# A two-layer encoder trunk with hierarchical MoE: the layer's first unit beside the ten weight slots, routing in one pass, and column halves for the last two down units

## What is computed

```python
def hierarchical_moe(h, norm_g, w_group, b_group, w_router, b_router, w_gate_up, w_down):
    xt = rms_norm(h, norm_g).reshape(B * S, D)
    g_prob = softmax(xt @ w_group + b_group)            # 4 groups
    g_idx = argmax(g_prob); g_w = g_prob[g_idx]
    e_logits = (xt @ w_router + b_router).reshape(-1, 4, 8)[g_idx]
    top_p, top_i = top_k(softmax(e_logits), 2)          # two experts of that group
    top_p = top_p / sum(top_p)
    gates = one_hot(g_idx * 8 + top_i) * (g_w * top_p)
    for each of the 32 experts:
        a, b = split(xt @ w_gu)                         # w_gu 1024 x 1024
        acc += ((silu(a) * b) @ w_d) * g                # w_d  512 x 1024
```

## Time and profile before

| | |
|---|---|
| median of 3 runs | 1136.43 us (1135.44 to 1140.93) |
| the profiled execution, its own time | 1138.69 us |
| its span in the profile | 1136.9 us |
| mean granted clock of TensorE, share of full | 0.976 |
| busy: PE, DVE, ACT, POOL | 89%, 21%, 15%, 5% |
| read from memory | 428.94 MB |
| largest groups of PE | L899 (gate and up) 2048 records, L933 (down) 1024 records |

### The profile page before, as it was taken

The page is one execution under the profiler, slowest core; times in us unless marked ns, Lnnn a source line. Parts: engine busy times, 40 slices in busy tenths (PEclk is TensorE's granted clock), DMA queues, the critical chain, the costliest instruction groups (busy, mean ns, idle before and its releaser), DMA issues.

```text
span 1136.9 us, 11377 instructions
## 1 busy us (share of the span) xinstructions
PE 1009.1 (89%) x4810; PEld 437.8 (39%) x4810; DVE 240.7 (21%) x527; ACT 171.1 (15%) x430; POOL 60.2 (5%) x94
## 2 busy tenths in 40 slices
PE   7999998989797989879799999979898989797986
PEld 6884532323232323223264654332323223232321
DVE  6992420101010010101035614101010101010101
ACT  3865300100000000000044503000000000000000
POOL 2890000000000000000000000000000000000000
PEclk9999999999999999999999999999999999899999
DMA  9794699999999999999996656999999999999996
GB/s 312 208 361 159 233 425 426 429 426 429 427 429 427 427 430 426 429 426 428 405 370 215 206 189 272 429 428 428 427 429 425 429 427 428 427 429 428 428 421 261
DMA packets 65006, 430.72 MB, mean 379 GB/s; under 512 B 12102, under 2 KB 22429, under 8 KB 44220
## 3 DMA queue, kind: packets, MB, share of 16 engines
q1 hardware_dynamic: 64830, 429.86, 92.8%
q10 hardware_dynamic: 126, 0.14, 0.0%
HBM read 428.94 MB, written 1.05 MB: 378 GB/s over the span
## 4 chain that ended last, share of the span: by engine, by line
PE 49%; DMA 45%; SPq 2%; ACT 1%; DVE 1%; issue 1%; DVEq 0%
DMA ring<-in_w_gate_up_dram 17%; DMA ring<-in_w_down_dram 15%; PE bank L899 12%; PE bank L933 10%; DMA zone<-in_w_gate_up_dram 10%; PE bank L789 5%; PE bank L880 5%; DMA zone<-in_w_down_dram 4%; PE bank L948 3%; PE bank L1130 2%; PE bank L829 2%; SPq L420 2%; PE bank L1027 1%; PE bank L1049 1%; PE bank L801 1%; PE bank L1004 1%
## 5 line engine op out<-in xcount | busy, mean ns | idle before, releaser
L899 PE MATMUL bank<-ring,zone 128*32 128x512 f32 x1184 | 336.0, 612 | 48.9 <-DMA ring<-in_w_gate_up_dram 30.8
L899 PE MATMUL bank<-zone 128*32 128x512 f32 x864 | 266.7, 611 | 33.4 <-DMA zone<-in_w_gate_up_dram 18.5
L933 PE MATMUL bank<-ring,xT 128*32 128x512 f32 x704 | 169.4, 622 | 20.0 <-DMA ring<-in_w_down_dram 14.3
L899 PEld LDWEIGHTS bank<-ring,zone 128*32 128x32 f32 x1184 | 87.7, 113 | 233.5 <-issue 233.1
L899 PEld LDWEIGHTS bank<-zone 128*32 128x32 f32 x864 | 68.3, 112 | 152.1 <-issue 152.1
L1348 DVE TENSOR_TENSOR xT<-xT,bank 128x512 f32<-128x512 f32 x16 | 11.0, 687 | 486.3 <-PE bank L899 486.3
L933 PE MATMUL bank<-zone,xT 128*32 128x512 f32 x320 | 96.3, 593 | 4.9 <-ACT xT L640 2.4
L1353 DVE TENSOR_TENSOR h<-bank,h 128x512 f32<-128x512 f32 x64 | 44.2, 691 | 259.6 <-PE bank L948 259.6
L638 ACT ACTIVATE xT<-bank 128x512 f32<-128x512 f32 x16 | 9.6, 597 | 563.5 <-PE bank L899 563.5
L933 PEld LDWEIGHTS bank<-ring,xT 128*32 128x32 f32 x704 | 44.7, 113 | 109.7 <-issue 90.3
L880 PEld LDWEIGHTS bank<-zone,xn 128*128 128x128 f32 x512 | 58.4, 192 | 13.3 <-issue 13.3
(11 more groups left out here) (247 smaller groups left out, 627.8 us busy)
## 6 DMA issues: line engine op xcount, KB each, us to landing
ring<-in_w_gate_up_dram SPq DMA_DIRECT2D x74, 2048.0 KB, 36.1
zone<-in_w_gate_up_dram SPq DMA_DIRECT2D x54, 2048.0 KB, 36.3
ring<-in_w_down_dram SPq DMA_DIRECT2D x44, 2048.0 KB, 36.7
zone<-in_w_down_dram SPq DMA_DIRECT2D x20, 2048.0 KB, 36.8
ring<-in_a_pw_w_dram SPq DMA_DIRECT2D x8, 1024.0 KB, 11.9
ring<-in_a_pw_w_dram SPq DMA_DIRECT2D x2, 2048.0 KB, 11.2
ring<-in_w_o_dram SPq DMA_DIRECT2D x2, 2048.0 KB, 20.9
ring<-in_w_uq_dram SPq DMA_DIRECT2D x1, 2304.0 KB, 13.0
```

Of the source, the lines that this page charges most:

```text
L899: ins = nc.tensor.matmul(bank[b][s * CAP:(s + 1) * CAP, :], xs[:, k, s * CAP:(s + 1) * CAP], rhs[:, b * HALF:(b + 1) * HALF], start=(k == ...
L933: ins = nc.tensor.matmul(bank[2 + b][s * CAP:(s + 1) * CAP, :], hidT[:, k, s * CAP:(s + 1) * CAP], rhs[:, b * HALF:(b + 1) * HALF], start= ...
```

## The change

- **The first unit outside the slots.** Unit 0 of each layer (the first 4 KB piece of the rows of all four experts) is loaded into four other places of 1024 columns: two in `xT`, `y_sb`, and a new tile `spare`. Unit 10 takes its slot and is issued in its place; the order is 10, 1 to 9, 0. Before unit 0 SP waits for the logits. DVE waits for the use of unit 0 before it writes to `xT`. `spare` also holds, at other times, what had tiles of its own: taps of the convolution, mask, router weights of layer 0, small arrays of the attention. The mask is now written by POOL in the attention, and DVE waits for it.
- **Units 4 to 11 of quad 0 by blocks** instead of by rows.
- **Routing.** Group logits lie as a fifth row of eight beside the four groups' experts (padded with a very low number). One pass finds the best of each of the five rows, a second one the second best of the four groups; the group's one-hot then selects. The first quad's one-hot is made from the places without the subtraction. The five keep-awake matmuls become 3 in layer 0 and 4 in layer 1.
- **The end of a layer.** The last quad's units 10 and 11 are each loaded in two column halves of 1 MB (pieces of 2 KB), both first halves before both second ones. The PE takes the first half of the columns of both, then unit 10's second half, scatters the first half, then unit 11's second half, and scatters that. In every quad the scatter goes by column halves first. Norm and transposes behind layer 0 and the first product of the attention follow the order of halves.

The core of the diff:

```diff
+        AHEAD = [SLOTS] + list(range(1, SLOTS)) + [0]
...
-        def by_blocks(n):
-            return n != 0
+        def by_blocks(n, u):
+            return n != 0 or u >= 4
...
+        first_unit = [xT_flat[:, 0:D], xT_flat[:, D:2 * D], y_sb, spare[:, :]]
...
+            def tail_dma(l, u, ex, hf):
+                r0 = (u - GU) * P
+                src = a["w_down"][l][bass.ds(ex, SIDE), r0:r0 + P, hf * HALF:(hf + 1) * HALF].rearrange("e p c -> p e c")
+                sp.dma_start(unit_sb[slot_last(l, u)][:, :, hf * HALF:(hf + 1) * HALF], src
+                             ).then_inc(E[l]["tail_in"] if hf == 0 else E[l]["unit_in"][slot_last(l, u)], 16)
...
-                for g in range(EARLY):
-                    if g < SLOTS:
-                        first(g)
+                for g in AHEAD + list(range(SLOTS + 1, EARLY)):
+                    if g == 0:
+                        sp.wait_ge(logits_done, 2 * l + 2)
+                        for s in range(SIDE):
+                            src = a["w_gate_up"][l][s, 0:HALF, :].rearrange("(p k) c -> p k c", k=4)[:, 0, :]
+                            sp.dma_start(first_unit[s], src).then_inc(first_in, 16)
+                        continue
+                    if g <= SLOTS:
+                        first(g % SLOTS)
...
+                        if u < UNITS - 2:
+                            unit_dma(l, slot_last(l, u), u, (i + (QUADS - 1)) % QUADS * SIDE, u < GU)
+                    for hf in range(2):
+                        for u in (UNITS - 2, UNITS - 1):
+                            tail_dma(l, u, (i + (QUADS - 1)) % QUADS * SIDE, hf)
...
-                keep_awake(5)
+                keep_awake(3 + l)
...
+                        if first and half == 0:
+                            for k in range(4):
+                                unit = landed(k)
+                                sides = unit if k == 0 else [unit[:, s, :] for s in range(SIDE)]
+                                chunk(sides, k, range(SIDE)).then_inc(e["used"], 1)
+                            continue
...
+                def down_last(n, landed, i):
+                    pe.wait_ge(e["hidT_ready"], n + 1)
+                    for k in range(KF - 2):
+                        unit = landed(GU + k)
+                        for b in range(2):
+                            ins = down_rows(k, b, unit)
+                        ins.then_inc(e["used"], 1)
+                    pe.wait_ge(e["tail_in"], 32 * i + 32)
+                    for k in (KF - 2, KF - 1):
+                        ins = down_rows(k, 0, unit_sb[slot_last(l, GU + k)])
+                    ins.then_inc(e["half_done"], 1)
+                    down_rows(KF - 2, 1, landed(UNITS - 2)).then_inc(e["used"], 1)
+                    scatter(n, 0)
+                    down_rows(KF - 1, 1, landed(UNITS - 1)).then_inc(e["used"], 1)
+                    scatter(n, 1)
...
-                link(V.tensor_reduce(gmx[:, :], lg[:, :, 0:G], AX_X, ALU.max))
-                V.tensor_tensor(gex[:, :, :], lg[:, :, 0:G], over(gmx[:, :], G), ALU.subtract).then_inc(gexp_in, 1)
-                link(V.tensor_tensor(geq[:, :, :], lg[:, :, 0:G], over(gmx[:, :], G), ALU.is_equal))
...
+                def top_of(values, top, hit, index, hot, n):
+                    im = iota_m[:, 0:EG].unsqueeze(1).to_broadcast([P, n, EG])
+                    link(V.tensor_reduce(top, values, AX_X, ALU.max))
+                    link(V.tensor_tensor(hit, values, over(top, EG), ALU.is_equal))
+                    link(V.tensor_tensor(hit, hit, im, ALU.mult))
+                    link(V.tensor_reduce(index, hit, AX_X, ALU.min))
+                    link(V.tensor_tensor(hot, im, over(index, EG), ALU.is_equal))
...
+                top_of(rows(lg[:, :, :, :]), row(mx[:, :, :]), rows(seq[:, :, :, :]), row(eix[:, :, :]), rows(oh1[:, :, :, :]), NRW)
+                link(V.scalar_tensor_tensor(out=em[:, :, :, :], in0=oh1[:, :, 0:G, :], scalar=-2 * NEG, in1=lg[:, :, 0:G, :],
+                                            op0=ALU.mult, op1=ALU.add))
...
+                top_of(rows(em[:, :, :, :]), row(mx2[:, :, :]), by_group(eeq), ix2, by_group(oh2), NGR)
...
+                link(V.tensor_tensor(picked_by_group, oh1[:, :, 0:G, :], oh2[:, :, :].rearrange("p t (g x) -> p t g x", g=G), ALU.add))
+                V.tensor_tensor(picked_by_group, picked_by_group, oh1[:, :, G, 0:G].unsqueeze(3).to_broadcast([P, TT, G, EG]),
+                                ALU.mult).then_inc(mask_ready, 1)
+                V.tensor_tensor(gex[:, :, :], lg[:, :, G, 0:G], over(mx[:, :, G], G), ALU.subtract).then_inc(exp_in, 1)
+                V.tensor_tensor(vm[:, 0, :, :], mx[:, :, 0:G], oh1[:, :, G, 0:G], ALU.mult)
+                link(V.tensor_tensor(vm[:, 1, :, :], mx2[:, :, :], oh1[:, :, G, 0:G], ALU.mult))
...
-                link(V.tensor_scalar(slot[:, :, 0:NE], eeq[:, :, :], -1.0, None, ALU.add))
...
+                    numbers, at = (iota_1, eeq) if first else (iota, slot)
...
-                    if not first:
+                    if first:
+                        dve.wait_ge(e["used"], 1)
+                    else:
                         dve.wait_ge(e["back_done"], n)
```

More of the change, by code:

```diff
@@ L662, in _ @@
             last = experts(0)
-            norm(2, E[0]["s_added"], 4 * last)
-            for b in range(4):
-                act.wait_ge(xT_ready, 8 + b + 1)
+            norm(2, E[0]["s_added"], 4 * last, (3, 4))
+            for i, b in enumerate(BY_HALF):
+                act.wait_ge(xT_ready, 8 + i + 1)
                 t, kh = b // 2, b % 2
@@ new lines, in gate_up, with chunk @@
+                def gate_up(n, landed, first):
+                    def chunk(rhs, k, sides):
+                        for b in range(2):
+                            for s in sides:
+                                ins = nc.tensor.matmul(bank[b][s * CAP:(s + 1) * CAP, :], xs[:, k, s * CAP:(s + 1) * CAP],
+                                                       rhs[s][:, b * HALF:(b + 1) * HALF], start=(k == 0), stop=(k == GU - 1))
+                            if b == 0 and k == GU - 1 and s == SIDE - 1:
+                                ins.then_inc(e["gate_done"], 1)
+                        return ins
+                    pe.wait_ge(e["xs_ready"], 2 * n + 1)
+                    for half in range(2):
+                        if half == 1:
+                            pe.wait_ge(e["xs_ready"], 2 * n + 2)
+                        if first and half == 0:
[4 more added lines that the diff above has]
+                            continue
+                        for pair in range(2):
+                            sides = (2 * pair, 2 * pair + 1)
+                            units = {s: landed(4 * half + s) for s in sides}
+                            for k in range(4):
+                                ins = chunk({s: units[s][:, k, :] for s in sides}, 4 * half + k, sides)
+                            ins.then_inc(e["used"], 2)
@@ L935, in down @@
                                 if b == 0 and k == KF - 1 and s == SIDE - 1:
                                     ins.then_inc(e["half_done"], 1)
-                        ins.then_inc(e["used"], 2 if blocks else 1)
-                def scatter(n, first):
-                    pe.wait_ge(e["pwT_ready"], n + 1)
-                    for j in range(4):
-                        t, hf = j // 2, j % 2
-                        if t == 0:
-                            pe.wait_ge(e["y_ready"], 2 * n + (hf + 1))
-                        if not (first and j < 2):
-                            pe.wait_ge(e["s_added"], 4 * n + (j - 1))
-                        nc.tensor.matmul(bank[6 + j % 2][:, :], pwT[:, t * P:(t + 1) * P], y_sb[:, hf * HALF:(hf + 1) * HALF],
+                        ins.then_inc(e["used"], 2)
@@ new lines, in scatter @@
+                def scatter(n, hf, first=False):
+                    if hf == 0:
+                        pe.wait_ge(e["pwT_ready"], n + 1)
+                    pe.wait_ge(e["y_ready"], 2 * n + (hf + 1))
+                    for t in range(TT):
+                        if not (first and hf == 0):
+                            pe.wait_ge(e["s_added"], 4 * n + (2 * hf + t - 1))
+                        nc.tensor.matmul(bank[6 + t][:, :], pwT[:, t * P:(t + 1) * P], y_sb[:, hf * HALF:(hf + 1) * HALF],
@@ L959, in last_landed, with quad @@
                     return unit_sb[slot_last(l, u)]
-                def quad(n, landed, first=False, end=False, ahead=True):
-                    gate_up(n, landed, not first)
+                def quad(n, landed, first=False, ahead=True, turn=None):
+                    gate_up(n, landed, first)
                     if ahead:
                         gather(n + 1)
-                    hidden_across(n, not first and not end)
+                    hidden_across(n, turn is None)
                     weights_back(n)
-                    down(n, landed, not first and not end)
+                    if turn is not None:
```

(6 more changed lines are left out.)

255 lines of the change are left out of this document (127 added, 128 removed).

## The result

The changed kernel took 1132.07 us (median of 7, 1128.70 to 1133.48), the kernel before 1137.18 beside it (7 runs). The ratio is 0.9947, with a 95% interval of 0.9931 to 0.9964: 4 to 8 us less. I had said 1127.7 against 1136.43, so 8.7 us less. The profiled execution of after took 1128.70 us, the fastest of its seven, and its span is 1127.0 us.

A forecast was written before the change was run, and what follows sets the result against it. Bytes over rate bound the full stretches; gains lie where the queue runs dry at layer starts and at layer ends. 0.9 + 1.2 + 4.2 + 2.4 = 8.7 us off the median 1136.43 gives 1127.7 us, range 1122 to 1134.

The forecast's parts named there:

- only the tails: Rival, chance 0.18: both layer starts give 0 instead of 5.1 us together, leaving 3.6 us gained, 1132.8 us.
- Layer 0's start: Routing and first unit outside the slots, layer 0: unit 11 lands 0.9 us sooner; 2.4 at full clock, -0.8 if late.
- the routing's gain is worth nothing here: Layer 0: the gather comes 2.3 us sooner, but the PE then idles 3.5 us for the first unit.
- The yardstick: Landing of unit 11 in each layer, after which the queue is full; coming earlier equals the gain of the layer's start.
- Layer 1's start: Layer 1: unit 11 lands at 707.9 instead of 712.1, 4.2 us sooner; bounds 2.8 and 5.2.
- Layer 1's end: Column halves at the end of layer 1: 2.4 us gained, the last byte coming 0.76 us later.
- Layer 0's end: Column halves at the end of layer 0: 1.2 us gained, between 1.5 and 0.8.
- a low clock on the first halves leaves 0.8: Layer 0's end: first scatter still running when the last half lands, so 0.8 us gained instead of 1.5.
- Quad 0 by blocks at no cost: Units 4 to 11 of quad 0: 14 us more PE work, gone after two quads, costed at nothing.
- The picks 1.2 us sooner: Sign in the routing: the picks end at 129.9 instead of 131.07, 1.2 us sooner.
- Last add 8 us earlier: Sign that the forecast is right: the kernel's last add comes 8 us earlier.
- The slower rival: Rival, chance 0.04: quad 0 frees slots too late, unit 14 is 3 us late, 1148 us.

The follow-up runs named there:

- the repeat: The changed kernel run once more, unchanged, in a later group: 1130.47 us, ratio 0.9932 to the kernel before, which took 1137.95 beside it.

## Why the prediction was right or wrong

The forecast of 1127.7 is 4.4 us under the median; the 1132.07 lies inside the range of 1122 to 1134. It lies closer to the 1132.8 of the rival "only the tails", but that is chance: this rival gives the starts nothing, and layer 1's start gave 4.1. By the ledger 8.7 us forecast stand against 7.0 and 7.2 in two profiles, and 5.1 and 7.5 in two pairs of medians.

**Layer 0's start, 0.9 forecast, -0.2 and 0.0 measured. This is the step that was mis-sized.** Its mechanism held: an idle of 3.5 us was forecast and 3.70 came, the first unit ran slowly, and "the routing's gain is worth nothing here" is what the run with late picks shows, down to "it may even cost". The yardstick was the landing of unit 11. For before I had worked it out as 152.9; its rows give the same:

```profile
141.55 0.37 SPq L420 DMA_DIRECT2D ring<-in_w_down_dram  x1
...
DMA to landing us min/median/max: 11.4/11.4/11.4
```

That is 30.8 us after unit 9's issue. After, unit 11 lands 22.92 + 7.6 = 30.5 us after it, and the forecast said 152.0 - 122.1 = 29.9. So the gain at the yardstick is 0.3, and it fades: unit 21 lands 80.9 us after unit 9's issue before and 80.7 after, and at the end of the layer nothing is left. Three pieces were too hopeful. I let units 8 and 9 come 0.4 us sooner in 16 KB pieces, but unit 9 landed 12.3 us after its issue as before. The first unit was ready 17.53 us after unit 9's issue, where I had 17.0. And it took 3.2 us at the low level and unit 1 2.2 (142.10 - 139.91) before unit 11 could go, together 5.4 where I had 3.4 + 1.73 = 5.1: the low level reached into the next unit. The gather came 2.0 us sooner where I had 2.3 (before's places start at 131.90, not at the 132.07 that I took), and the idle swallowed it. A larger omission: I never set this part against leaving the unit in its slot. That comparison is 2.2 us in favour of the slot, and it would have shown in my own numbers, where PE stands still for 3.5 us only because of the unit outside.

**Layer 1's start, 4.2 forecast, 4.1 and 4.3 measured.** I had the first unit 14.4 us after unit 9's issue and it came after 13.92; unit 11's issue at 18.0 came at 17.62, landing after 7.9 (7.8 forecast). The picks' 1.4 measured 1.35 to 1.5, the unit outside the rest, 2.7. The rival of the tails alone fails here.

**Layer 1's end, 2.4 forecast, 2.6 and 2.5 measured.** The 2 KB pieces ran at the rate I took, 386 GB/s from 554 to 558 and from 1110 to 1115 against the 384 of the earlier trace rows, and counted from the landing of the last gate and up unit the last byte came 0.6 and 0.5 us later than before, where I had 0.76. The line rate from 512 B up that the Trainium skill states (DMA: Bandwidth & Descriptors, section "Specifications"), weighed in the prediction, is not met: 16 KB pieces ran at 427 to 429. The measurement decides for the row.

**Layer 0's end, 1.2 forecast, 0.5 measured** in both profiles of the change, and 1.1 to 1.3 in six others, where the first halves ran at the full clock (26.54 to 26.67 against 27.80). That is the case "a low clock on the first halves leaves 0.8", which I gave too little weight. The other side of it I had missed: by rows the last unit may run slowly as well, and then the halves save 2.0 to 3.9 us there (29.34 and 30.46 against 27.34 and 26.55).

**Quad 0 by blocks at no cost: right.** The share is 0.99 to 1.01 from 146 to 200, and going back to rows gained nothing. **The picks 1.2 us sooner: right**, 1.1. "Last add 8 us earlier": 7.0 by the common origin. The slower rival asked for 3 us of lateness at unit 14; it lands 45.2 us after unit 9's issue, where before has 46.6. The profiled pair's 9.95 us would have looked like a little more than the forecast; 2.93 of it is the scatter of the opening.

## What to carry to other kernels

When a buffer is moved off a full ring so that a later transfer can start earlier, its contents should be used last, not first: the move alone was worth about nothing in sum, and the changed order took another 9 to 10 us off. Before a chain is shortened, look at what waits at its end; if that is a transfer, the shorter chain only gathers the idle into one piece, and here the matmul engine that stood still for 3.7 us in one piece paid for it with its clock. Split two profiles into stages from a common event before reading their difference, and set each step against leaving that step alone out, not only against the kernel before.

## What the runs showed of the hardware

- The granted clock near the edge: after an idle of 2.71 us the first halves of layer 0 took 4.48 us for 24 records (window 559 to 564: 0.66), after 2.67 us those of layer 1 took 1.92 for 16, in the same execution. Idles of 2.7 us fall either way; those of 3.70, 3.74 and 4.80 were followed by matmuls at the low level each time, those of 0.80, 1.12 and 1.29 by matmuls at the full clock. One of 1.81 was followed by the full clock, one of 1.84 by the low level: with the picks late in layer 0, the filler behind the places took 2.06 us instead of 1.10. And the clock was low without an idle too: right behind the logits the repeat's six keep-awake records took 4.50 us, the changed kernel's 2.82. So the length of one idle doesn't settle the level.
- A slow stretch spreads: 2.2 us more waiting in layer 1 cost 4.0, since the places and the gather behind it ran at 3.15 and 5.05 instead of 1.80 and 3.81 us.
- Four transfers of 512 KB in 4 KB pieces, queued behind others, landed 9.7 to 12.1 us after their issue in layer 0 and 6.2 to 8.9 in layer 1; a 2 MB unit issued when nothing else was on its way, after 7.3 to 8.5.
- The start of the program takes one of two lengths, with the same code (119.18 and 121.82 to unit 9's issue in two profiles of the changed kernel). In the five long ones of thirteen the PE works at half the pace from 12 to 15 us.
